# Hybrid diffusion backbone with a routed mixture of experts: six modulation pieces computed in the first output projection, two fixed experts in both layers, router weights as the stationary operand

## What is computed

```python
mod_l = jax.nn.silu(c) @ w_ada[layer] + b_ada[layer]
sh1, sc1, g1, sh2, sc2, g2 = split(mod_l, 6)
mod_c = jax.nn.silu(c_ctx) @ w_ada[layer] + b_ada[layer]   # for the context, same split
...
x_lat = x_lat + g1 * o_l
f_l = rms_norm(x_lat, g_ffn[layer]) * (1.0 + sc2) + sh2
...
scores = jax.nn.sigmoid(tokens @ w_router)          # (T, 32)
sel = scores + b_router                             # best of 4 groups of 8, two best experts in it
g_idx = argmax(sum of the two best of each group)
e_idx = top_k(sel inside that group, 2)
gate = normalised scores of the two
y[expert e] = (silu(x @ w1[e]) * (x @ w3[e])) @ w2[e]
x_lat = x_lat + g2 * sum_k gate_k * y_k
```

## Time and profile before

| | us |
|---|---|
| median of 3 runs (lowest, highest) | 3283.02 (3279.16, 3284.39) |
| profiled execution, its own time | 3282.2 |
| its span | 3280.3 |
| TensorE matmul busy in the span | 2946.8 (90%) |
| VectorE busy | 1517.2 (46%) |
| ScalarE busy | 1067.6 (33%) |
| GpSimd busy | 503.7 (15%) |
| mean granted TensorE clock | 0.946 of full |

### The profile page before, as it was taken

One profiled execution on the slowest core, in us unless ns is written; L12 is line 12 of the kernel. 1 busy time (PEld: TensorE's weight loads), 2 busy tenths in 40 slices (PEclk: granted clock), 3 DMA queues, 4 the chain that ended last, 5 costly groups with the idle time before them and its releaser, 6 DMA issues. The chain is left out here.

```text
span 3280.3 us, 73136 instructions
## 1 busy us (share of the span) xinstructions
PE 2946.8 (90%) x27967; PEld 1896.0 (58%) x27967; DVE 1517.2 (46%) x4558; ACT 1067.6 (33%) x2406; POOL 503.7 (15%) x802
## 2 busy tenths in 40 slices
PE   6999976889999879999995999899998969999895
PEld 3777644845545447767563455477776535566552
DVE  2333346855555442222223688666666452222223
ACT  1111112456631113323223344355553112223222
POOL 0000002600033022323221000000002003222223
PEclk8999986989999889999997999899999979999998
DMA  9500057500032299999995222200002359999998
GB/s 344 205 26 26 13 184 245 131 1 1 1 117 102 80 392 406 414 415 414 415 400 184 82 90 71 77 1 1 1 1 111 142 197 391 415 415 416 415 416 310
DMA packets 163151, 661.77 MB, mean 202 GB/s; under 512 B 22388, under 2 KB 34852, under 8 KB 113764
## 3 DMA queue, kind: packets, MB, share of 16 engines
q1 hardware_dynamic: 132932, 564.30, 44.0%
q0 software_dynamic: 19424, 63.98, 5.3%
q10 hardware_dynamic: 10560, 30.16, 2.4%
HBM read 576.72 MB, written 81.66 MB: 201 GB/s over the span
## 5 line engine op out<-in xcount | busy, mean ns | idle before, releaser
L2630 PE MATMUL ps_g<-w_ring,work 128*32 128x256 f32 x9600 | 567.1, 386 | 52.8 <-DMA w_ring<-in_w 44.4
L2630 PEld LDWEIGHTS ps_g<-w_ring,work 128*32 128x32 f32 x9600 | 360.5, 111 | 226.6 <-issue 68.3
L2718 DVE STREAM_TRANSPOSE work<-work 128x256 f32<-128x256 f32 x189 | 123.8, 655 | 681.5 <-PE ps_g L2630 667.9
L2684 ACT COPY work<-ps_y 32x256 f32<-32x256 f32 x760 | 276.4, 364 | 287.8 <-PE ps_y L2645 281.0
L2645 PE MATMUL ps_y<-w_ring,work 128*32 128x256 f32 x4864 | 296.9, 382 | 3.4 <-ACT work L2684 3.4
L1715 PE MATMUL of_ps_r<-w_early,cat 128*128 128x512 f32 (+1 forms) x608 | 256.9, 579 | 3.0 <-ACT cat L1798 3.0
L430 PE MATMUL ps_r<-w,hT 128*128 128x512 f32 (+1 forms) x640 | 249.8, 546 | 1.5 <-ACT hT L489 1.5
L2645 PEld LDWEIGHTS ps_y<-w_ring,work 128*32 128x32 f32 x4864 | 185.3, 111 | 85.2 <-ACT work L2684 4.3
L2589 POOL DMA_INDIRECT work<-f_dram,ex_idx x200 | 194.4, 972 | 157.5 <-POOL ex_idx L2586 155.9
L2678 ACT ACTIVATE work<-ps_g 128x128 f32<-128x128 f32 x192 | 53.5, 278 | 485.8 <-PE ps_g L2630 479.2
L1715 PEld LDWEIGHTS of_ps_r<-w_early,cat 128*128 128x128 f32 x608 | 115.3, 193 | 126.6 <-issue 122.9
(11 more groups left out here) (494 smaller groups left out, 4302.2 us busy)
## 6 DMA issues: line engine op xcount, KB each, us to landing
w_ring<-in_w SPq DMA_DIRECT2D x304, 1024.0 KB
w_early<-in_w SPq DMA_DIRECT2D x80, 1024.0 KB
y_dram<-work ACTq DMA_DIRECT2D x190, 128.0 KB
y_dram<-zeros POOLq DMA_DIRECT2D x2, 9216.0 KB, 45.0
ml_staging<-in_w_ada SPq DMA_DIRECT2D x9, 2048.0 KB
w_ring<-in_w_ada SPq DMA_DIRECT2D x6, 2048.0 KB, 19.9
ml_spare<-in_w_ada SPq DMA_DIRECT2D x5, 2048.0 KB
ml_arena<-ml_rows SPq DMA_DIRECT2D x40, 256.0 KB, 4.3
```

The costliest lines, as they stand in the source:

```text
L2630: mm = pe.matmul(ps_h[rows, :], xT[:, k * UNIT:(k + 1) * UNIT], w[:, :, kk * DE + n * P:kk * DE + (n + 1) * P], start=k == 0, stop=k == KD ...
L2684: w = act.copy(y[b * UNIT:(b + 1) * UNIT, n * 256:(n + 1) * 256], ps_y[n * UNIT:(n + 1) * UNIT, :])
L2718: dve.transpose(xT.rearrange("p (k t) -> p k t", k=KD), xs.rearrange("p (r k) -> p k r", k=KD)).then_inc(x_turned, 1)
```

## The change

Six pieces move from both `route` stages into `mix_out` of layer 0 (`M.late`), for the latent part alone. A piece is loaded into a tile of its own (`wa`), multiplied row by row by silu(c) and summed over the eight k on VectorE (`late`, 8 instructions), and one column of ones on TensorE sums it over partitions (4 matmuls). In both layers `FIXED` is 2: experts 0 and 1 come first; in layer 1 eight chunks (`EARLY_SLOTS`) are loaded in `mix_out`, and the other four, or in layer 0 all twelve, at the start of `route`. The router's weights are the stationary operand in four column groups; ScalarE copies the four partial sums (`parts_of`) and one matmul folds them (`fold`), one tile later.

```diff
-FIXED = (0, 1)
+FIXED = 2
-ROUTED = (range(NCHUNK - 6, NCHUNK - 2), range(NCHUNK - 2, NCHUNK))
+LAST = range(NCHUNK - 6, NCHUNK)
...
 @block.sync   (mix_out)
+                if M.late:
+                    ada_load(sp, A, M.late[0], wa[:, :, :], ada_in)
                 for n, (tile, kind) in enumerate(tiles):
                     sp.wait_ge(x_new, n + 1)
                     sp.dma_start(M.x_rows(tile), x[:, n % 4, :]).then_inc(x_st[n % 4], 16)
+                    if 1 < n <= len(M.late):
+                        sp.wait_ge(ada_mm, n - 1)
+                        ada_load(sp, A, M.late[n - 1], wa[:, :, :], ada_in)
                     sp.wait_ge(f_ready, n + 1)
...
 @block.tensor
                 def router(n):
                     pe.wait_ge(f_act, 2 * n + 2)
                     if n:
-                        pe.wait_ge(lg_ready, n)
+                        pe.wait_ge(parts_out, n)
...
-                    for k in range(KD):
-                        mm = pe.matmul(ps_r[:, 0:NE], fT[:, k, :], wr[:, k, :], start=k == 0, stop=k == KD - 1)
+                    if 0 < n <= len(M.late):
+                        pe.wait_ge(ada_sum, n)
+                        for m in range(4):
+                            at = P + 4 * (n - 1) + m
+                            mm = pe.matmul(ps_r[:, at:at + 1], wa[:, 0, m * P:(m + 1) * P], g.ones[:, 0:1], start=True, stop=True)
+                        mm.then_inc(ada_mm, 1)
+                    for r in range(2):
+                        for j in range(4):
+                            k = 4 * r + j
+                            mm = pe.matmul(ps_r[NE * j:NE * j + NE, 0:P], wr[:, k, :], fT[:, k, :], start=r == 0, stop=r == 1)
                     mm.then_inc(r_done, 1)
+                def fold(n):
+                    pe.wait_ge(parts_out, n + 1)
+                    if n:
+                        pe.wait_ge(lg_ready, n)
+                    pe.matmul(ps_l[:, 0:NE], parts[:, :], g.consts[:, FOLD:FOLD + NE], start=True, stop=True).then_inc(l_done, 1)
...
 @block.scalar
+                def parts_of(n):
+                    act.wait_ge(r_done, n + 1)
+                    if n:
+                        act.wait_ge(l_done, n)
+                    act.copy(parts[:, :], ps_r[:, 0:P]).then_inc(parts_out, 1)
...
 @block.vector
+                def late(j):
+                    dve.wait_ge(ada_in, 16 * (j + 1))
+                    dve.tensor_scalar(wa[:, 0, :], wa[:, 0, :], g.cs[:, 0, 0:1], None, ALU.mult).then_inc(*c.up())
+                    for k in range(1, KD):
+                        own()
+                        w_sum = dve.scalar_tensor_tensor(out=wa[:, 0, :], in0=wa[:, k, :], scalar=g.cs[:, k, 0:1], in1=wa[:, 0, :], op0=ALU.mult, op1=ALU.add)
+                        w_sum.then_inc(*(c.up() if k < KD - 1 else (ada_sum, 1)))
...
-                    if n:
-                        scores(n - 1)
+                    if n > 1:
+                        scores(n - 2)
+                    if 0 < n <= len(M.late):
+                        late(n - 1)
...
-    M.early = FIXED[1] * CHUNKS
+    M.early, M.late = min(FIXED * CHUNKS, EARLY_SLOTS), ()
...
 @block.sync   (route)
-        for n, q in enumerate(chunks):
-            ada_load(sp, A, q, wa[n], ada_in[n])
+        for q in range(early, fixed * CHUNKS):
+            load_chunk(sp, A, layer, R, q // CHUNKS, q // CHUNKS, q % CHUNKS)
         sp.wait_ge(R.tabled, 1)
...
 @block.tensor   (route: product and turn are gone)
-        product(0)
         pe.wait_ge(ranked, 1)
...
-    turned = np.array([int(f"{p:05b}"[::-1], 2) for p in range(NE)], np.float32)
+    spread = [int(f"{p:05b}"[::-1], 2) for p in range(NE)]
+    turned = list(range(FIXED)) + [r for r in spread if r >= FIXED]
```

More of the change, by code:

```diff
@@ L1580, in even_mix @@
     M.halves = (None, lambda t: L.hb[:, t, :])
-    M.early = 0
+    M.early, M.late = 0, LAST
     return M
@@ L2233, in odd_mix, with route @@
     M.halves = (lambda t: L.cat[:, t, 0:CW], lambda t: L.cat[:, t, CW:])
-    M.early = FIXED[1] * CHUNKS
+    M.early, M.late = min(FIXED * CHUNKS, EARLY_SLOTS), ()
     return M
-def route(nc, g, A, layer, R, nt, block):
+def route(nc, g, A, layer, R, nt, early, block):
     tag = f"rt{layer}_"
     n, m = nt * NE, nt * NG
-    fixed = FIXED[layer]
+    fixed = FIXED
     def s(name):
@@ L2271, in route @@
     c = Count(nc, tag + "dve_step")
[L2272 to L2280, removed]
+    R.tabled, R.listed = s("tabled"), s("listed")
     consts, assigned, counted, ranked, sorted_, based, base_in, low_in, list_mm = (
@@ L2294, in _ @@
             pool.iota(ap, pattern=pattern, base=base_at, channel_multiplier=step, allow_small_or_imprecise_dtypes=True).then_inc(consts, 1)
[L2296 to L2301, removed]
-            act.copy(mrow[:, n % 2, :], ps_mod[n % 2]).then_inc(ada_row, 1)
     @block.sync
     def _(sp):
-        for n, q in enumerate(chunks):
-            ada_load(sp, A, q, wa[n], ada_in[n])
+        for q in range(early, fixed * CHUNKS):
+            load_chunk(sp, A, layer, R, q // CHUNKS, q // CHUNKS, q % CHUNKS)
         sp.wait_ge(R.tabled, 1)
@@ L2338, in _ @@
         pe.matmul(ps_d[:, 0:NE], spread2[0:NE, :], g.ident[0:NE, 0:NE], start=True, stop=True).then_inc(base_in, 1)
-        turn(0)
-        for j in range(1, min(3, len(chunks))):
-            product(j)
-        for j in range(1, min(3, len(chunks))):
-            turn(j)
         pe.wait_ge(low_in, 1)
@@ L2350, in _ @@
         mm.then_inc(list_mm, 1)
-        for j in range(3, len(chunks)):
-            product(j)
-            turn(j)
     @block.vector
@@ L2361, in _ @@
         dve.memset(ones_e[:, :], 1.0).then_inc(*c.up())
-        dve.memset(lead[:, :], float(LEAD)).then_inc(*c.up())
+        for e in range(fixed):
+            dve.memset(lead[:, e:e + 1], float(LEAD * (fixed - e) + e)).then_inc(*c.up())
         for q in range(P // UNIT):
@@ L2404, in _ @@
         own()
-        for part, last in ((slice(0, fixed), lead[:, :]), (slice(fixed, NE), number[:, fixed:NE]))[1 - fixed:]:
+        for part, last in ((slice(0, fixed), lead[:, :]), (slice(fixed, NE), number[:, fixed:NE]))[0 if fixed else 1:]:
             dve.scalar_tensor_tensor(out=code[:, part], in0=count[:, part], scalar=float(NE), in1=last, op0=ALU.mult, op1=ALU.add).then_inc(*c.up())
@@ L2837, in ffn @@
             R.ps_l = nc.alloc_psum_tensor(f"ps_l{layer}", [P, 512], F32)
[L2838 removed]
+            R.ps_g = nc.alloc_psum_tensor(f"ps_g{layer}", [P, 512], F32)
             with nc.Block() as block:
[L2840 removed]
+                route(nc, g, A, layer, R, nt, M.early, block)
                 experts(nc, g, A, layer, M, R, block)
```

64 lines of the change are left out of this document (32 added, 32 removed).

## The result

The changed kernel's median is 3262.57 us (3258.32 to 3271.70, 7 runs), against 3284.36 (3279.16 to 3287.00, 7 runs) of the kernel before on the same chip: a ratio of 0.9940, 95% interval 0.9927 to 0.9952, so 16 to 24 us faster. 3269 was predicted, inside a range of 3256 to 3284. The profiled execution took 3262.42 us, with a span of 3260.4.

What follows compares the result with a forecast made beforehand. DMA was taken to bound both expert stages once the ring turns, TensorE `mix_out`. Terms -8.9 + 7.2 - 2.0 - 10.4 = -14.1 us against the profiled 3282.2 gave 3268.1, so a median of 3269, range 3256 to 3284.

Steps and rivals of the forecast that it cites:

- Router and fold: Layer 1's `mix_out` and tail: router 0.5 us instead of 1.80, fold +0.23 us, in all -8.9 us.
- seven routers and six folds inside the stage: Layer 1's `mix_out`: routers save 9.1 us and folds cost 1.4 us, giving -7.7 us.
- The six pieces: Layer 0's `mix_out`: load-and-sum cycles on VectorE make the stage 8.0 us longer, +7.2 us with the tail.
- VectorE frees `ps_o` at 1013.1, and `out(3)` ends at 1026.9: Layer 0's `mix_out`, behind the first piece: `out(3)` ends 7.0 us later than before.
- The two engines side by side: Layer 0's `mix_out`, first piece: each of seven VectorE sums beside GpSimd costs 0.7 us more, +4.9 us.
- Routes: Both `route` stages: with the product gone, -1.6 us in layer 1 and -0.4 in layer 0, -2.0 in all.
- Experts 0: Layer 0's experts: a first expert of 4 rounds instead of 6 frees the first slot earlier, -10.4 us.
- All 20 chunks are there when TensorE starts: Layer 0's experts: 20 chunks loaded from 1141.9 take 51 us, so are there at about 1193.
- Experts 1 and the early chunks: Layer 1's experts: expert 0 stays first and two early chunks count for nothing, 0 us.
- Rival (b): Layer 0's `mix_out`: the pieces hide, stage at -0.4 us, sum -21.7, 3261 us; chance 0.18.
- Rival (d): Layer 0's `mix_out`: a load-and-sum cycle longer by 2.8 us takes the gain, by 4.1 makes it slower; chance 0.12.
- Rival (c): Layer 0's experts: the new order gives nothing, sum -3.7, 3279 us; chance 0.13.

Runs made afterwards that it cites:

- run 1: The changed kernel with layer 0's experts in the order of before (none fixed, largest first, chunks loaded after the table); 3271.97 us, 0.9966 of before.
- run 5: The changed kernel with expert 1 first and expert 0 second in both layers; 3256.41 us, 0.9926 of before.
- run 6: The changed kernel with no chunk loaded in layer 1's `mix_out`, all twelve at the head of its routing; 3263.03 us, 0.9937 of before.
- run 11: The changed kernel, unchanged, for a second profile; 3262.15 us (one run).
- run 8: Run 3 with all products of pieces behind the two small matmuls that VectorE waits for; 3247.29 us, 0.9896 of before.
- run 7: The changed kernel with the pieces back in the routings and the router as before, only the two fixed experts staying; 3267.31 us, 0.9964 of before.
- run 3: The changed kernel with the six pieces back in the two routings, new router, fold and two fixed experts kept; 3247.83 us, 0.9891 of before.
- run 4: The changed kernel with the six pieces in tiles 3 to 8 instead of 1 to 6; 3248.12 us, 0.9899 of before.
- Run 10: The kernel before with the table of constants 32 columns wider, the new columns unused; 3273.82 us, 0.9989 of before.
- run 2: The changed kernel with the router as before, no partial sums and no fold, pieces in `mix_out`; 3285.89 us, 1.0013 of before.

## Why the prediction was right

- **Router and fold, right.** Predicted 0.5 us for the router and 0.23 for the fold, measured 0.57 and 0.14. `mix_out` 1 gave -6.6 instead of -7.7: the step "seven routers and six folds inside the stage" counts one of each too many, since the seventh router stands behind the last `out` (2632.12); with six and five the prediction's own figures give -6.65. The tails gave 1.2 and 1.0 us (end of `out` to the first matmul of `route`), forecast as 1.2. From the router's first record to the next `out`, with a change of tiling at either end, it is 0.57 us for 16 records, 0.036 each against the 0.033 of the earlier trace rows; there is no room for 0.26 us twice. By the Trainium skill, TensorEngine Tiling (Array Packing), Key Properties, a change of the tiling mode drains TensorE; no run here shows a price of it.
- **The six pieces: +9.5 against +8.0, by the path that the prediction named.** The instructions beside GpSimd were forecast at 11.0 us and took 11.4; the last sum came 73.1 us after the stage's first matmul, 73.0 in the forecast. From there the five cycles of load and sum, forecast at 17.8 us, took 18.0: a piece landed 12.1 us behind the tile's first operation on average (11.7 forecast), since its load alone took 9.4 us and not 8.4. That is 1.1 of the 1.5 us missing. Beside this path stood a step that failed: "VectorE frees `ps_o` at 1013.1, and `out(3)` ends at 1026.9" runs TensorE at full clock behind the stall. It had waited 9.45 us and came back at 0.50, so `out(3)` ended 10.5 us late instead of 7.0. It was luck that this did little harm. VectorE's chain was behind TensorE's at full clock, and its cycles are longer than TensorE's own 17.38 us, so by the last piece it had used up nearly all of the 3.5 us: the first operation behind the last sum starts at 1096.43, and TensorE's product at 1096.67. In the five profiles of kernels with this stage as changed (after and runs 1, 5, 6, 11), the last sum is ready only 0.1 to 0.9 us before the product. A TensorE at full clock would by these rows have waited for the sums instead; that is argued, and no run tests it.
- **The two engines side by side.** The seven sums beside GpSimd cost 0.66 us each more than alone, near the 0.7 taken. In the trace they and GpSimd's instructions end in turns, and a sum takes 0.98 us beside GpSimd's shorter instruction and 1.4 to 1.65 beside a longer one, against 0.78 alone. A wait for a whole instruction each time, which is the most that a full block as the Trainium skill has it (SBUF — State Buffer, Terms) could cost, would have been up to 1.26; the turns fit the rule, and the price is smaller.
- **Routes, right.** From the first matmul of `route` to the first expert matmul 1.0 and 2.3 us were gained, against 0.4 and 1.6. The product is gone, but TensorE still waits 1.57 and 1.66 us in front of the sort matmul, released by VectorE's queue; run 8 shows that products beside the sort cost 1.0 and 0.3 us.
- **Experts 0, right in size (-11.6 against -10.4), with the cause split.** Run 1 puts 9.4 us on the order where no piece is in the queue, run 7 8.1 on it where four are. The pieces in the queue cost nothing that stands out of the scatter with the old order, whose first slot comes free 30 us after the first expert matmul, and 4 us with the new one, where it is 20 (run 3). The prediction had no term for this: its -10.4 needs "All 20 chunks are there when TensorE starts" and the first freed slots to be what the queue waits for, and so needs the pieces gone. The dry stretch was some 16 us, forecast as 18. A slip without effect: 98 rounds of 5.18 us from 1191.6 end at 1699, not 1703.
- **Experts 1 and the early chunks, right.** -0.8, and run 6 takes all eight early chunks away at no cost.
- **Rival (b)**, the pieces hidden, gave 3261 us, nearer to the measured 3262.57 than the forecast's 3269, and yet it is not what happened: `mix_out` 0 did not give its -0.4, and for its landing 9.4 us after the tile's first operation 11.3 to 13.2 were measured. Behind the first piece TensorE waited for a sum in one tile, 0.66 us; run 4 is near the kernel that (b) describes. **Rival (d)** needed a cycle of 17.8 + 2.8 us; the mean was 18.0 and the longest 19.1. **Rival (c)** fell with run 1.
- **The remainder.** The measured ratio asks for 16 to 24 us, the edited stages show 14.4 to 15.1. What is missing to the middle, 5 us, lies in stages whose lengths vary by up to 8 us between profiles. The prediction had no term for them. Run 10 makes the place of the tiles behind the constants a likely part of it (0.7 to 6.9 us by its interval), without settling it.

The parts do not add up to a good change everywhere. By runs 3 and 4 the move of the pieces, as written, costs 16 and 14 us against doing without it or starting it two tiles later; run 3, with router and order but not the move, gains 1.09% where the whole change gains 0.60%. The prediction's own terms said so (its +7.2 held some 10 us of the router's gain) and it drew no conclusion from them. Runs 3, 4 and 8 beat both kernels, by 1.0 to 1.1% against before, and can't be told apart.

## What to carry to other kernels

Work that "moves into idle time" of an engine should be asked which other engine is busy beside it just then and who stands behind it: two tiles later the same six pieces cost 1 us a tile and one stall of 1.4 us instead of one of 9.45. A delay on one engine can be used up by another engine's longer chain behind it, so compare the two at the end of the stage and not at the stall alone. A dry load queue is free room: before traffic is moved out of it, weigh what it leaves behind, for some 16 of the 20 us of traffic were hidden there. When a ring starts to turn, count the sum of the rounds in front of each release and not only of the first one, since one release moved forward alone (run 5) bought at most 1.9 us in layer 0 and 3.5 in layer 1 of its 5.2.

## What the runs showed of the hardware that was not expected

- TensorE's granted clock fell without a wait of more than 0.35 us: an eight-record product of one column (1 us) and a 16-record router of 32 columns (1.8 us) in a row were followed by a granted clock of 0.67 over 5.2 us of `out`; four tiles of five with both in run 2 show such a fall. The product with the 0.6 us router (changed kernel) and the old router without a product (kernel before) left it at 1.00; what in the pair brings it down was not tested. After 1.36 us of waiting in run 4 it was 0.74:

```profile
1082.40:1087.10 4.70, 4.70 (x12) 2.13 (x9) 2.96 (x17) 1.39 (x4) 0.00 (x0) 0.74 0.76 242
```

- A router whose weights are stationary in 32-column groups, between two neighbours of full tiling, took 0.57 us for its 16 records, 0.036 each, against 0.033 in a stretch without such a change.
- Stages without an edited instruction, ahead of `mix_out` 0, end anywhere within 8 us (930.9 to 938.8) in thirteen profiles, two of them with the narrower table of constants; a single pair of profiles can't carry a claim of 5 us about them.
